# Block-wise inverse of two scan directions: the second direction laid across the halves of TensorE's array, its products issued beside those of the first

## The reference

```python
def gated_delta_rule_chunked(q, k, v, g, beta):
    ...
    decay = jnp.where(incl, jnp.exp(jnp.where(incl, gdiff, 0.0)), 0.0)
    kb = k * beta[..., None]
    L = jnp.where(strict, jnp.einsum('bhncd,bhnmd->bhncm', kb, k) * decay, 0.0)
    eye = jnp.eye(CHUNK, dtype=jnp.float32)
    T = lax.linalg.triangular_solve(eye + L, jnp.broadcast_to(eye, L.shape), left_side=True,
                                    lower=True, unit_diagonal=True)
    u = jnp.einsum('bhncm,bhnme->bhnce', T, v * beta[..., None])
    w = jnp.einsum('bhncm,bhnmd->bhncd', T, kb * jnp.exp(g)[..., None])
    ...
def first_block(...):
    for l in range(DEPTH):
        ...
        y_a = diff_attention(...)
        y_b = gated_deltanet(...)
        ...
        x = x + gt1 * (merged @ w_out[l])
        h = rms_norm(x, norm2_g[l]) * (1.0 + sc2) + sh2
        x = x + gt2 * (jnp.square(jax.nn.relu(h @ w_mlp1[l])) @ w_mlp2[l])
```

## Time and profile before

| | us |
|---|---|
| median of 2 runs | 2196.24 |
| range of these | 2194.28 to 2198.19 |
| the profiled execution, its own time | 2194.73 |
| its span in the profile | 2193.3 |

### The profile page before, as it was taken

How to read it: one execution, slowest core, us unless ns; L and a number is a source line. 1 busy time by engine, 2 the same in 40 slices (tenths; PEclk the granted TensorE clock), 3 DMA queues, 4 the chain that set the end, 5 groups by cost and what they waited for, 6 DMA issues and landing times.

```text
span 2193.3 us, 31044 instructions
## 1 busy us (share of the span) xinstructions
PE 1880.5 (86%) x12852; PEld 1255.4 (57%) x12852; DVE 913.0 (42%) x1536; ACT 634.0 (29%) x1098; POOL 43.2 (2%) x46
## 2 busy tenths in 40 slices
PE   6999999999999999999898866666798996756666
PEld 3887888987888889988655311112275552212112
DVE  3675576645576576646753100000068530000001
ACT  3244235545245136534451100000055310000001
POOL 0001000000002000000000000000000000000000
PEclk9999999999999999999999978888899999788778
DMA  9565348556533354453658999999983789999997
GB/s 337 213 231 193 117 154 307 193 192 224 198 129 142 117 177 169 187 196 66 236 204 351 427 427 425 429 426 427 420 267 128 306 358 426 427 427 425 429 425 330
DMA packets 120006, 617.50 MB, mean 282 GB/s; under 512 B 18448, under 2 KB 21434, under 8 KB 86586
## 3 DMA queue, kind: packets, MB, share of 16 engines
q1 hardware_dynamic: 119290, 613.85, 70.7%
q10 hardware_dynamic: 576, 1.66, 0.2%
HBM read 614.44 MB, written 1.05 MB: 281 GB/s over the span
## 4 chain that ended last, share of the span: by engine, by line
PE 59%; DMA 28%; DVE 9%; ACT 2%; issue 1%; SPq 0%; POOL 0%; DVEq 0%; ACTq 0%
PE pb L706 57%; DMA ring<-in_w_up_dram 17%; DMA ar<-in_w_up_dram 4%; DMA hT<-in_w_up_dram 4%; PE pb L709 2%; DVE ar L1639 2%; DVE ar L1647 2%; DMA ring<-in_w_down_dram 1%; DVE small L1655 1%; DMA ring<-in_ada_w_dram 1%; DVE ar L1643 1%; DVE ar L1651 1%; ACT ar L2441 1%; DVE small L1643 0%; DVE ws L1639 0%
## 5 line engine op out<-in xcount | busy, mean ns | idle before, releaser
L706 PE MATMUL pb<-ring,ar 128*32 128x512 f32 (+1 forms) x2128 | 360.9, 726 | 185.0 <-DMA ring<-in_w_up_dram 140.7
L706 PE MATMUL pb<-ar 64*64 64x64 f32 (+10 forms) x3760 | 438.1, 372 | 74.5 <-DMA hT<-in_w_up_dram 35.9
L2445 ACT COPY ar<-pb 128x512 f32<-128x512 f32 (+2 forms) x195 | 112.7, 578 | 920.5 <-PE pb L706 868.5
L1651 DVE COPY ar<-pb 128x512 f32<-128x512 f32 (+5 forms) x98 | 58.7, 599 | 722.2 <-PE pb L706 707.7
L706 PEld LDWEIGHTS pb<-ar 64*64 64x64 f32 (+5 forms) x3760 | 212.0, 144 | 242.2 <-issue 224.0
L706 PEld LDWEIGHTS pb<-ring,ar 128*32 128x32 f32 (+1 forms) x2128 | 96.6, 132 | 396.2 <-issue 385.3
L706 PE MATMUL pb<-hT,ring 128*128 128x256 f32 x1024 | 235.4, 386 | 0.4 <-ACT ar L2441 0.4
L706 PEld LDWEIGHTS pb<-hT,ring 128*128 128x128 f32 x1024 | 193.0, 192 | 33.6 <-issue 7.8
L1639 DVE TENSOR_TENSOR ws<-ring,ws 128x1024 fp32r<-128x1024 f32 x128 | 156.9, 1226 | 124.0 <-ACT ws L2445 122.2
L706 PE MATMUL pb<-hs,ws 128*128 128x256 f32 x1536 | 187.0, 284 | 2.5 <-ACT aux L2445 1.5
L706 PEld LDWEIGHTS pb<-hs,ws 128*128 128x128 f32 x1536 | 185.6, 193 | 4.3 <-ACT aux L2445 1.7
(11 more groups left out here) (168 smaller groups left out, 1647.9 us busy)
## 6 DMA issues: line engine op xcount, KB each, us to landing
ring<-in_w_down_dram SPq DMA_DIRECT2D x46, 2048.0 KB, 27.8
ring<-in_w_gate_dram SPq DMA_DIRECT2D x42, 2048.0 KB, 28.4
ring<-in_w_up_dram SPq DMA_DIRECT2D x40, 2048.0 KB, 23.4
ring<-in_w_mlp_dram SPq DMA_DIRECT2D x32, 2048.0 KB, 7.7
ring<-in_w_in_dram SPq DMA_DIRECT2D x27, 2048.0 KB, 9.2
ring<-in_ada_w_dram SPq DMA_DIRECT2D x24, 2048.0 KB, 8.5
ar<-in_w_gate_dram SPq DMA_DIRECT2D x12, 2048.0 KB, 20.4
ar<-in_w_up_dram SPq DMA_DIRECT2D x12, 2048.0 KB, 23.2
```

The lines of the kernel that those rows point to most:

```text
L706: return e.matmul(o, l, r, start=start, stop=stop)
L1651: return e.tensor_copy(o, i)
L2445: return e.copy(o, i)
```

## The change

The data of direction 1 are laid across: its `X` and `AT` now sit in the other half of the partitions (chunk in partitions 0 to 63 before, in 64 to 127 now), `XT` and `B` stay. A product from one half of the partitions into the other half of the PSUM bank uses the other two corners of the array. A function `chunks` now takes one or two products and interleaves them matmul by matmul, each into a PSUM bank of its own. Direction 1 is shifted by half a level, so that a product of direction 0 stands beside one of direction 1:

- `d_X`: X0 of both directions, together.
- `d_B(s)`: B of direction 0 at level s, together with dX of direction 1 at level s - 1; `d_T(s)`: dXT of direction 1 at level s - 1, alone.
- `d_U(s)`: dX of direction 0 at level s, together with B of direction 1 at level s; `d_V(s)`: dXT of direction 0, alone.

POOL needs `LT` of direction 1 in swapped halves for its `AT`. That is a new step, `d_swap`: PE waits for `V("LT", l, 1)`, multiplies `LT` of direction 1 by the identity into the other halves (2 matmuls of 64x64 by 512), and ACT copies the result to `LT_swap`. It stands right behind `("d_LT", 1)` in both tables. ACT's scaled keys KD move with the copy of B of direction 1, from `d_B(2)`, `d_B(3)` to `d_U(2)`, `d_U(3)`.

```diff
-        ("d_decay", 1), ("r", 4), ("d_LT", 0), ("d_LT", 1), ("r", 5), ("r", 6), ("f", 25, 0), ("r", 7), ("f", 25, 1),
+        ("d_decay", 1), ("r", 4), ("d_LT", 0), ("d_LT", 1), ("d_swap",), ("r", 5), ("r", 6), ("f", 25, 0), ("r", 7), ("f", 25, 1),
...
-            def chunks(name, l, key, lhs, rhs, by, what):
+            def chunks(l, *products):
+                pbs = [bank(name, l, *key)[1] for name, key, lhs, rhs, across, by, what in products]
                 for t in range(2):
                     for h in range(4):
-                        for pp in halves:
-                            o = 256 * t + 64 * h
-                            m = mm(pb[pp, o:o + 64], lhs[pp, t, h, :], K("eye")[pp, :] if rhs is None else rhs[pp, t, h, :])
+                        o = 256 * t + 64 * h
+                        for (name, key, lhs, rhs, across, by, what), pb in zip(products, pbs):
+                            for n, pp in enumerate(halves):
+                                m = mm(pb[halves[1 - n] if across else pp, o:o + 64], lhs[pp, t, h, :],
+                                       K("eye")[pp, :] if rhs is None else rhs[pp, t, h, :])
+                            if (t, h) == (1, 3):
+                                m.then_inc(*P.up(name, l, *key))
...
+            def d_swap(l):
+                e.wait_ge(*V("LT", l, 1))
+                k, pb = bank("LT_swap", l)
+                for n, pp in enumerate(halves):
+                    m = mm(pb[halves[1 - n], :], K("eye")[pp, :], LT[pp, 1].rearrange("p t h c -> p (t h c)"))
+                m.then_inc(*P.up("LT_swap", l))
+                psum.until(k, A, "LT_swap", l)
...
+            def B_of(l, s, i):
+                e.wait_ge(*G("AT", l, s, i))
+                e.wait_ge(*(A("X0", l, i) if s == 1 else V("X", l, s - 1, i)))
+                return "B", (s, i), AT[:, i], X[:, i], i == 1, A, "B"
+
+            def dX_of(l, s, i):
+                e.wait_ge(*A("B", l, s, i))
+                e.wait_ge(*V("XT", l, s - 1, i))
+                return "dX", (s, i), XT[:, i], B[:, i], i == 1, V, "X"
...
             def d_B(l, s):
-                for i in range(2):
-                    e.wait_ge(*G("AT", l, s, i))
-                    e.wait_ge(*(A("X0", l, i) if s == 1 else V("X", l, s - 1, i)))
-                    chunks("B", l, (s, i), AT[:, i], X[:, i], A, "B")
+                if s == 1:
+                    chunks(l, B_of(l, 1, 0))
+                else:
+                    chunks(l, B_of(l, s, 0), dX_of(l, s - 1, 1))
+
+            def d_T(l, s):
+                chunks(l, dXT_of(l, s - 1, 1))
 
             def d_U(l, s):
-                for i in range(2):
-                    e.wait_ge(*A("B", l, s, i))
-                    e.wait_ge(*V("XT", l, s - 1, i))
-                    if s < 5:
-                        chunks("dX", l, (s, i), XT[:, i], B[:, i], V, "X")
-                    chunks("dXT", l, (s, i), B[:, i], XT[:, i], V, "XT")
+                if s < 5:
+                    chunks(l, dX_of(l, s, 0), B_of(l, s, 1))
+                else:
+                    chunks(l, B_of(l, 5, 1))
+
+            def d_V(l, s):
+                chunks(l, dXT_of(l, s, 0))
...
             def d_B(l, s):
-                for i in range(2):
-                    e.wait_ge(*P("B", l, s, i))
-                    copy(whole(B[:, i]), ps("B", l, s, i)[:, :]).then_inc(*A.up("B", l, s, i))
+                B_copy(l, s, 0)
+
+            def d_U(l, s):
+                B_copy(l, s, 1)
                 if s in (2, 3):
                     keys(l, "KD", s - 2)
...
-                        a8, l8 = (z[:, i].rearrange("p t h c -> p (t h) c") for z in (AT, LT))
+                        if s == 1 and i:
+                            e.wait_ge(*A("LT_swap", l))
+                        a8 = AT[:, i].rearrange("p t h c -> p (t h) c")
+                        l8 = v4(LT_swap, 8) if i else LT[:, 0].rearrange("p t h c -> p (t h) c")
```

More of the change, by code:

```diff
@@ L1030, in d_LT @@
                 psum.until(k, V, "LT", l, t)
-            def chunks(name, l, key, lhs, rhs, by, what):
-                k, pb = bank(name, l, *key)
+            def chunks(l, *products):
+                pbs = [bank(name, l, *key)[1] for name, key, lhs, rhs, across, by, what in products]
                 for t in range(2):
                     for h in range(4):
-                        for pp in halves:
-                            o = 256 * t + 64 * h
-                            m = mm(pb[pp, o:o + 64], lhs[pp, t, h, :], K("eye")[pp, :] if rhs is None else rhs[pp, t, h, :])
-                m.then_inc(*P.up(name, l, *key))
-                psum.until(k, by, what, l, *key)
+                        o = 256 * t + 64 * h
[5 more added lines that the diff above has]
+                                m.then_inc(*P.up(name, l, *key))
+                for name, key, lhs, rhs, across, by, what in products:
+                    psum.until(psum.at[(name, l, *key)], by, what, l, *key)
+            def d_swap(l):
[5 more added lines that the diff above has]
+                psum.until(k, A, "LT_swap", l)
             def d_X(l):
@@ L1963, in d_LT, with X_less, XT_less, d_B @@
                         tt(x8, bc(K("eye").unsqueeze(1), [128, 8, 64]), x8, ALU.subtract).then_inc(*V.up("XT", l, 0, i))
-            def d_U(l, s):
-                for i in range(2):
[L1967 to L1972, removed]
-                    tt(x8, x8, ps("dXT", l, s, i)[:, :], ALU.subtract).then_inc(*V.up("XT", l, s, i))
+            def X_less(l, s, i):
+                e.wait_ge(*P("dX", l, s, i))
+                x8 = X[:, i].rearrange("p t h c -> p (t h c)")
+                tt(x8, x8, ps("dX", l, s, i)[:, :], ALU.subtract).then_inc(*V.up("X", l, s, i))
+            def XT_less(l, s, i):
+                e.wait_ge(*P("dXT", l, s, i))
+                x8 = XT[:, i].rearrange("p t h c -> p (t h c)")
+                tt(x8, x8, ps("dXT", l, s, i)[:, :], ALU.subtract).then_inc(*V.up("XT", l, s, i))
+            def d_B(l, s):
+                if s > 1:
+                    X_less(l, s - 1, 1)
+            def d_T(l, s):
+                XT_less(l, s - 1, 1)
+            def d_U(l, s):
+                if s < 5:
+                    X_less(l, s, 0)
+            def d_V(l, s):
+                XT_less(l, s, 0)
             def d_uw(l, i):
@@ L2645, in d_X, with d_swap, B_copy @@
                     copy(whole(X[:, i]), ps("X0", l, i)[:, :]).then_inc(*A.up("X0", l, i))
+            def d_swap(l):
+                e.wait_ge(*P("LT_swap", l))
+                copy(LT_swap, ps("LT_swap", l)[:, :]).then_inc(*A.up("LT_swap", l))
+            def B_copy(l, s, i):
+                e.wait_ge(*P("B", l, s, i))
+                copy(whole(B[:, i]), ps("B", l, s, i)[:, :]).then_inc(*A.up("B", l, s, i))
             def d_B(l, s):
-                for i in range(2):
-                    e.wait_ge(*P("B", l, s, i))
-                    copy(whole(B[:, i]), ps("B", l, s, i)[:, :]).then_inc(*A.up("B", l, s, i))
+                B_copy(l, s, 0)
+            def d_U(l, s):
+                B_copy(l, s, 1)
                 if s in (2, 3):
@@ L2698, in scalar @@
                          d_conv=d_conv, d_silu=d_silu, d_tok=d_tok, d_gate=d_gate, d_gcum=d_gcum, d_l2=d_l2, d_kqT=d_kqT,
-                         d_decay=d_decay, d_LT=d_LT, d_X=d_X, d_B=d_B, d_uw=d_uw,
+                         d_decay=d_decay, d_LT=d_LT, d_swap=d_swap, d_X=d_X, d_B=d_B, d_U=d_U, d_uw=d_uw,
                          d_hn1=lambda l: head_square("yb", l, O, zone(ZTOK + 1024, 1024), V("o", l, 1, 1)))
```

22 lines of the change are left out of this document (14 added, 8 removed), and 3 rows, old and new, of the table k.

## The result

| | before | after |
|---|---|---|
| median of 2 runs, us | 2196.24 | 2212.49 |
| range, us | 2194.28 to 2198.19 | 2210.01 to 2214.97 |
| the profiled execution, its own time | 2194.73 | 2214.97 |
| its span | 2193.3 | 2213.7 |

The ratio is 1.0082, with a 95% interval of 1.0065 to 1.0098: slower by 0.8%. The forecast was 2210, by its case A.

A forecast was written before the change was run, and what follows sets the result against it. PE was taken to bound the first block; 14.1 (swap) - 5.7 (inverses) + 4.4 (clock, long waits) + 1.7 (clock, short wait) = +14.5 us, giving 2210 us, 0.6% slower, range 2201 to 2223.

The forecast's parts named there:

- case A: Whole kernel: the forecast itself, slower at 2210 us, own range 2203 to 2218; 70%.
- Part 3: Swap ahead of the inverses: PE waits 7.8 us (layer 1) and 4.5 (layer 0), swaps cost 1.8; sum +14.1 us.
- Part 4: Clock lost after PE idles: two long waits at the swap +4.4 us, one short wait in the inverses +1.7 us.
- Part 1: Products of the inverses: a pair on four corners takes one product's 0.93 us, PE falls from 30 to 21 slots.
- rival B: Inverses: four corners don't work beside each other, a pair takes 1.87 us; 2221 to 2223 us; 15%.
- Part 2: Inverses: ways back over ACT and DVE show, with waits for ACT's keys; 26.4 and 30.5 us, together -5.7 us.
- rival D: Inverses: pairs work and the instruction stream can't keep up, or the clock stays low throughout; up to 2230 us; 5%.
- the keys' wait: Inverses: PE waits 2.0 us more for ACT's keys after `d_U(2)` and after `d_U(3)`, 4.0 us for each layer.
- +1.7 of Part 4: Inverses: of four waits of 2.0 us, one is counted as losing the clock, +1.7 us (bounds 0 and 6.8).
- C: Second block: the DMA-bound end swallows the first block's delay, so not slower, about 2195 us; 10%.

The follow-up runs named there:

- e7: Changed kernel with later swap, inverse matmuls except X0 halved in number and 128 columns wide (second head wrong), keys in blocks of 8: 2191.55 us, ratio 0.9982.

## Why the prediction was right, and which steps of it weren't

The number was right (2210 against 2212.5), the case too (A). Of its terms two hold and two don't, and part of the agreement is luck.

**Part 3 and the long waits of Part 4 hold.** Waits 7.8 and 4.5 forecast, 7.71 and 4.38 measured. Swap, wait and clock together: 14.1 + 4.4 = 18.5 forecast, 10.5 + 8.3 = 18.8 measured. The clock's part shows as 1.97 instead of 1.08 us for each swap (1.8 in all) and 2.7 us in the work behind, so 4.5. Taking the price of a lost clock from two other waits of the same kernel was good enough in the sum, though not for each: less wait and swap, 2.9 us are left in layer 0, behind the shorter wait, and 1.7 in layer 1, and with the swap alone the same long wait left 2.8. The swap alone gives 2214 and the late swap 2194: this term is the whole loss.

**Part 1 holds.** The pair takes 0.93 us: in the kernel after the pair X0 starts at 708.99, and ACT's two copies of it at 710.18; less the 0.26 us from a product's end to its copy, the pair ended at 709.92. Read directly, its 64 records last 1.16 us and the 32 of one product alone 1.15. That refutes rival B. Its kernel would be that of the products in turn with the early swap: 6.3 us on top of 2212.5 makes 2218.8 (an estimate), and not B's 2221 to 2223, since a product in turn takes 0.87 us and not 0.93. Part 1 cites a rule of the Trainium skill ("TensorE: Matmul & The Clock Gate", Part 3, "The mechanism"), by which a weight load overlaps matmuls in flight only when its row group is another one, so that products side by side should take as long as in turn; these runs disagree with it for corners that share a row group (1.16 against 1.91 us).

**Part 2 is mis-sized.** It has 26.4 us for layer 1 and 30.5 for layer 0; the kernel after takes 30.3 and 31.6, so the term is -0.7 (-1.9 + 1.2) instead of -5.7. The step that failed is its first sentence, "with PE's time shorter, the way from a product over another engine back to PE shows": the next limit was not an engine but the arrival of PE's instructions, the first half of rival D, to which I gave 5% without working it out. The sentence ahead of Part 1, "before, nothing but PE's own rate counted", failed with it: the gap of 0.65 us at 209.65 in the trace of the kernel before, in the middle of a product and with no releaser, was there to be read. With half the instructions the lengths with keys in blocks are 26.5 and 30.2, those of Part 2 within 0.3 us, and without the keys' wait 23.1 where it has 22.4 (the 0.25 us more a round on DVE's way back is most of that). So the chain of waits was read rightly and stood behind another limit. The two agree by different routes, though (a product of wide matmuls takes 0.88 us, a round 4.22, and a clock loss takes the place of one of the keys' waits); the agreement to 0.3 us is in part luck.

**The +1.7 of Part 4 didn't occur.** The four waits of 2.0 us for the keys aren't there, since the gaps for instructions come earlier and let ACT catch up; what is left of them is 1.73 us at the longest, in this row of layer 0 of the kernel after:

```profile
229.42 3.20 PE L708 MATMUL pb<-ar 64*64 64x64 f32 x159 [1.73 <-ACT ar L2493]
```

The clock is 1.00 in both inverses. In e7, where the waits of 2.02 us do occur, one of three costs the clock.

**The sum** comes near because errors cancel. In its own terms it would have been 18.8 - 0.7 + 0 = +18.1 instead of +14.5, on the profiled execution 2212.8; that one took 2215.0. The 2.2 us between lie outside these terms: 0.7 are there ahead of kk in layer 0 already (193.99 against 193.32) and 1.8 arise behind the inverse of layer 1 (the parts add up to 0.3 more, by rounding); neither was traced further. The median of the two runs lies 2.5 us under the profiled execution, where it lay 1.5 above it before. So the forecast missed the profiled execution by 5.8 us (3.6 in its terms, 2.2 outside them), and 4.0 of these are taken back by where the two profiled executions lie among their runs. That is luck.

**C is refuted** by the swap alone: 19.7 us lost in the first block, 19.3 at the end. The DMA-bound stretch doesn't swallow them; the window from 1240 to 1580 us has PE busy for 228.1 us in the kernel after, against 220.9, with the DMA share at 1.01 in both. That fits the same work reached later.

**What stays open.** That instructions are short is shown by the halving, by the gaps' fixed places and by the packets that land ahead of them. What sets the rate is not. The packets are 0.9 to 1.5 us in flight; behind each of the four gaps of layer 1 the next packet starts 1.1 to 1.4 us after PE has resumed, as if it were asked for only then. Flight, the 1.2 to 1.5 us to PE's start and this delay make up the 3.8 us, but no run changed one of them. Nor is it shown why layer 1 takes 30.3 us in the kernel after and 28.7 with the late swap, with the same order of instructions from X0 on. The gaps stand at the same records but are longer (1.10 and 0.73 us against 0.28 and 0.19 for the first two), and the first packet of the inverse starts 2.0 us behind X0 instead of 1.0, so the fetch is 1 us late from the outset; what delays it isn't known.

## What to carry to other kernels

When small matmuls are put beside each other, divide the number of instructions by the time that is left for them before counting the gain: where PE already uses its instructions as fast as they come, work that overlaps better saves nothing, and only fewer and wider instructions do. Gaps without a releaser in the middle of a product, at the same record counts whenever they come, are the sign of it. A new step in an in-order queue costs what its operand is late by, plus the clock that is lost with the wait. The first can be read off the trace before, as the distance from the queue's place to the operand's last write; the second only roughly (1.7 to 2.9 us here). The same step a few entries later cost only its own 1.1 us.

## What the runs showed of the hardware

- PE in a stretch of 64x64 matmuls of 64 columns in float32 got 256 instructions (128 records with their weight loads) in about 3.8 us on average: 8 packets of 16 KB in 29 to 30 us with and without pairs. With pairs it had gaps of 0.6 to 1.14 us with no releaser, which ended 1.2 to 1.5 us after a packet had landed. With matmuls twice as wide 4 packets sufficed and these gaps were gone.
- Two products on four corners, interleaved by twos, last 1.16 us from first start to last end, as long as one alone (1.15); one after the other they last 1.91.
- Waits of 4.38 and 7.71 us each left PE at 1.2 GHz for 6.8 us, part of it still waiting; in the kernel with the swap alone the same wait of 7.71 us left it there for 10.2 us. Of three waits of 2.02 us one was followed by 3.4 us at 0.50, which began 1.0 us after work had resumed.
- From the signal of DVE's subtraction to the start of the matmul that waited for it last: mostly 0.15 us ahead of `d_B` (three semaphore waits) and 0.35 us ahead of `d_U` (six), in the kernels with interleaved pairs.
